# One diffusion block and two attention layers on one core: the opening's loads and waits in a new order, and the attention steps' order on VectorE and GpSimd changed

## What is computed

```python
def _ada(cvec, w_ada, b_ada):
    mod = jax.nn.silu(cvec) @ w_ada + b_ada
    return jnp.split(mod, N_MOD, axis=-1)

def _modulate(x, g, shift, scale):
    return _rmsnorm(x, g) * (1 + scale) + shift

def differential_attention(...):           # 4 heads of the second network, per block of 128 queries
    sc = jnp.einsum('bhcqd,bhckd->bhcqk', qi, k).astype(jnp.float32) * scale
    p = jax.nn.softmax(sc, axis=-1)
    a = p[:, :, 0] - lam * p[:, :, 1]      # two softmaxes, the second times lam, subtracted
    return jnp.einsum('bhqk,bhkd->bhqd', a, vf)
```

## Time and profile before

| | |
|---|---|
| median of 3 runs (lowest, highest) | 3914.33 us (3908.04 to 3921.22) |
| the profiled execution: its own time | 3913.21 us |
| the profiled execution: span | 3911.4 us |
| granted TensorE clock, mean of the span | 0.978 |
| PE busy | 93% |
| DVE, ACT, POOL busy | 29%, 20%, 11% |

### The profile page before, as it was taken

How to read it: one execution, slowest core, us unless ns; L and a number is a source line. 1 busy time by engine, 2 the same in 40 slices (tenths; PEclk the granted TensorE clock), 3 DMA queues, 4 the chain that set the end, 5 groups by cost and what they waited for, 6 DMA issues and landing times.

```text
span 3911.4 us, 33012 instructions
## 1 busy us (share of the span) xinstructions
PE 3627.2 (93%) x12600; PEld 1750.7 (45%) x12600; DVE 1151.3 (29%) x2612; ACT 767.0 (20%) x1772; POOL 428.8 (11%) x393
## 2 busy tenths in 40 slices
PE   8999999999999798788888788999999989999999
PEld 3555555444444433233332344555444545454444
DVE  3355656333201303110111034433221144432211
ACT  2135454223201200000000022222110122221100
POOL 0003324011000000000000002101220021012200
PEclk9899999999999899999999999999999999999999
DMA  8413223112224599999999961012222211122220
GB/s 282 154 61 97 87 72 103 49 56 87 65 65 178 212 409 409 409 409 409 409 409 409 409 236 54 27 44 81 85 76 74 76 54 38 38 92 77 74 81 27
DMA packets 302209, 634.08 MB, mean 162 GB/s; under 512 B 32554, under 2 KB 145818, under 8 KB 301798
## 3 DMA queue, kind: packets, MB, share of 16 engines
q1 hardware_dynamic: 241278, 592.28, 40.7%
q10 hardware_dynamic: 60776, 39.70, 3.7%
HBM read 625.50 MB, written 10.24 MB: 163 GB/s over the span
## 4 chain that ended last, share of the span: by engine, by line
PE 55%; DMA 17%; DVE 3%; SPq 1%; issue 1%; POOL 0%; ACT 0%; DVEq 0%
PE psum L308 27%; DMA arena<-in_w_exp_up_dram 7%; DMA arena<-in_w_exp_gate_dram 6%; PE psum L1638 6%; PE psum L2441 5%; PE psum L2898 4%; PE psum L2934 4%; DMA arena<-in_w_exp_down_dram 4%; PE psum L1462 2%; PE psum L2919 1%; PE psum L1490 1%; PE psum L2367 1%; PE psum L1471 1%; SPq L277 1%; PE psum L2833 1%
## 5 line engine op out<-in xcount | busy, mean ns | idle before, releaser
L308 PE MATMUL psum<-arena 128*128 128x512 f32 (+1 forms) x3200 | 1302.9, 565 | 2.6 <-POOL arena L2040 2.4
L308 PEld LDWEIGHTS psum<-arena 128*128 128x128 f32 x3200 | 609.8, 193 | 675.3 <-issue 653.0
L2441 PE MATMUL psum<-arena 128*64 128x512 f32 x3072 | 692.9, 597 | 141.7 <-DMA arena<-in_w_exp_up_dram 77.1
L2441 PEld LDWEIGHTS psum<-arena 128*64 128x64 f32 x3072 | 232.4, 136 | 583.3 <-issue 567.5
L1638 PE MATMUL psum<-arena 128*128 128x512 f32 x768 | 351.0, 612 | 0.0
L810 PE MATMUL psum<-arena 128*128 128x512 f32 (+1 forms) x768 | 255.9, 491 | 1.1 <-DVE arena L550 1.1
L1638 PEld LDWEIGHTS psum<-arena 128*128 128x128 f32 x768 | 147.0, 195 | 193.4 <-issue 192.5
L1570 DVE CUSTOM_DVE_ANT_0 arena<-psum,arena 128x512 f32<-128x512 f32 (+3 forms) x224 | 113.9, 546 | 391.2 <-PE psum L1462 391.0
L2977 POOL TENSOR_SCALAR arena<-arena 128x512 f32<-128x512 f32 x88 | 138.6, 1576 | 697.7 <-ACT arena L2956 697.7
L810 PEld LDWEIGHTS psum<-arena 128*128 128x128 f32 x768 | 144.4, 191 | 107.9 <-issue 96.1
L2983 DVE SCALAR_TENSOR_TENSOR arena<-arena 128x512 f32<-128x512 f32 x88 | 66.2, 752 | 426.5 <-POOL arena L2977 426.5
(11 more groups left out here) (276 smaller groups left out, 2909.4 us busy)
## 6 DMA issues: line engine op xcount, KB each, us to landing
arena<-in_w_exp_gate_dram SPq DMA_DIRECT2D x128, 1024.0 KB, 18.6
arena<-in_w_exp_up_dram SPq DMA_DIRECT2D x128, 1024.0 KB, 18.5
arena<-in_w_exp_down_dram SPq DMA_DIRECT2D x128, 1024.0 KB, 18.5
arena<-in_w_in_dram SPq DMA_DIRECT2D x64, 1024.0 KB, 5.2
arena<-in_w_up_dram SPq DMA_DIRECT2D x88, 512.0 KB, 4.9
arena<-in_w_ada_dram SPq DMA_DIRECT2D x24, 1024.0 KB, 9.1
arena<-in_w_down_dram SPq DMA_DIRECT2D x20, 1024.0 KB, 5.1
arena<-acs_scratch ACTq DMA_DIRECT2D x64, 256.0 KB, 4.6
```

The source lines that it names most:

```text
L308: mm = pe.matmul(shaped(b, l, r), l, r, start=kt == 0, stop=kt == nkt - 1)
L2441: mm = pe.matmul(banks[n][64 * j:64 * j + 64, :], lhs[:, kt, 64 * j:64 * j + 64], w, start=kt == 0, stop=kt == 2 * nkb - 1)
```

## The change

Opening: SP first loads the identity, then the first `w_ada` block (1, 0), the rest of the constants, `x` in two pieces (the second half first), `ctx`, and after them `w_ada` (0, 0). The four small vectors go to ACT's queue. PE waits for the identity alone before its first transpose, and does the product of (0, 0) after the transposes of `x`. DVE takes the columns of (1, 0) ahead of squaring `x`. Attention: in `dve_att_2`, `weights` stands before `scores`; in `pool_att_2`, `second` has lag 0, not 1. Both serve all three attentions, though `second` acts on differential units only.

```diff
--- before.py
+++ after.py
@@ -564,18 +564,21 @@
             for n in range(2):
                 turned(e, "c", jp, 2 * jp + n, PS.of(("HT", "c", jp))[:, 256 * n:256 * n + 256], HT[:, 2 * jp + n, 512:768], n == 1)
 
-        def sp_vec(sp, groups, key):
+        def load_vec(e, groups, key):
             for col, r, ap, n in vec_src:
                 if col in groups:
-                    sp.dma_start(stage[r:r + n, col * 128:(col + 1) * 128], ap).then_inc(*up(S(f"vec_in{groups[0]}"), by=16))
+                    e.dma_start(stage[r:r + n, col * 128:(col + 1) * 128], ap).then_inc(*up(S(f"vec_in{groups[0]}"), by=16))
             mark(key, S(f"vec_in{groups[0]}"))
 
         def sp_start(sp):
-            sp_vec(sp, (0,), ("vec", 0))
-            sp.dma_start(consts, csrc).then_inc(*up(S("consts_in"), ("consts",), by=16))
+            sp.dma_start(ident, csrc[:, 0:128]).then_inc(*up(S("ident_in"), ("ident",), by=16))
             sp_ada(sp, 1, 0)
+            sp.dma_start(consts[:, 128:], csrc[:, 128:]).then_inc(*up(S("consts_in"), ("consts",), by=16))
+            for i in (2, 0):
+                sp.dma_start(xin[:, i:i + 2, :], xT[:, i:i + 2, :]).then_inc(*up(S(f"x_in{i // 2}"), ("x_in", i), ("x_in", i + 1), by=16))
+            sp.dma_start(cin, A["ctx"].rearrange("a (t p) d -> p (a t) d", p=128)).then_inc(*up(S("c_in"), ("c_in",), by=16))
             sp_ada(sp, 0, 0)
-            sp_vec(sp, (1, 2, 3, 4, 5), ("vec", 1))
+            load_vec(sp, (1, 2, 3, 4, 5), ("vec", 1))
             sp_ada(sp, 1, 1)
             sp_ada(sp, 0, 1)
 
@@ -593,9 +596,7 @@
             act.activation(dst, src, ACT.Copy, bias=0.0, scale=ssq_of[nm][0][:, i:i + 1]).then_inc(*up(S("act_xn"), ("xn", nm, i)))
 
         def act_start(act):
-            for i in range(4):
-                act.dma_start(xin[:, i, :], xT[:, i, :]).then_inc(*up(S(f"x_in{i}"), ("x_in", i), by=16))
-            act.dma_start(cin, A["ctx"].rearrange("a (t p) d -> p (a t) d", p=128)).then_inc(*up(S("c_in"), ("c_in",), by=16))
+            load_vec(act, (0,), ("vec", 0))
             act.wait_ge(*at("col", 0))
             act.wait_ge(*at("cv0"))
             act.activation(cv3[:, :, 0], vmain[:, 56:64], ACT.Silu, bias=0.0, scale=1.0).then_inc(*up(S("act_cv")))
@@ -639,17 +640,17 @@
 
         def dve_start(dve):
             dve_vec(dve, 0)
+            dve_ada_copy(dve, 1, 0, r0bufs[0])
+            dve.wait_ge(*at("col", 0))
+            dve_ada_cols(dve, 1, 0, gpm)
             for i in (2, 3):
                 dve.wait_ge(*at("x_in", i))
                 dve_square(dve, "x", i, xin[:, i, :])
             dve_rstd(dve, "x", *ssq_of["x"], 1024.0)
-            dve_scaled(dve, "x", 0, xin[:, 0, :], xn_x[:, 0, :])
-            dve_ada_copy(dve, 1, 0, r0bufs[0])
-            dve_scaled(dve, "x", 2, xin[:, 2, :], xn_x[:, 2, :])
+            for i in (0, 2):
+                dve_scaled(dve, "x", i, xin[:, i, :], xn_x[:, i, :])
             dve.wait_ge(*at("c_in"))
             dve_square(dve, "c", 1, cin[:, 1, :])
-            dve.wait_ge(*at("col", 0))
-            dve_ada_cols(dve, 1, 0, gpm)
             dve_rstd(dve, "c", *ssq_of["c"], 1024.0)
             dve_scaled(dve, "c", 0, cin[:, 0, :], xn_c[:, 0, :])
             dve_ada_copy(dve, 0, 0, r0bufs[1])
@@ -673,14 +674,15 @@
             pe_turn(pe, ("vec", i), PALL, [stage[0:vec_n[i], i * 128:(i + 1) * 128]], "pe_turn")
 
         def pe_start(pe):
-            pe.wait_ge(*at("consts"))
+            pe.wait_ge(*at("ident"))
             pe.wait_ge(*at("vec", 0))
             pe_vec(pe, 0)
             pe.wait_ge(*at("cv"))
             pe_ada_product(pe, 1, 0)
-            pe_ada_product(pe, 0, 0)
+            pe.wait_ge(*at("consts"))
             pe_ada_cols(pe, 1, 0, r0bufs[0])
             pe_turned_x(pe, 0)
+            pe_ada_product(pe, 0, 0)
             pe_ada_cols(pe, 0, 0, r0bufs[1])
             pe_ada_product(pe, 1, 1)
             pe_turned_c(pe, 0)
@@ -1618,7 +1620,7 @@
                 dve.scalar_tensor_tensor(out=oT2[:, p, :], in0=PS.of(("o2", J.id, p)), scalar=J.gain, in1=hy, op0=ALU.mult, op1=ALU.mult).then_inc(
                     *up(S("dve_oT"), ("free", ("o2", J.id, p)), ("oT2", J.id, p)))
 
-            yield from att2_steps(J, (1, sums), (0, scores), (1, weights), (2, turned), (3, outs), (4, heads))
+            yield from att2_steps(J, (1, sums), (1, weights), (0, scores), (2, turned), (3, outs), (4, heads))
 
         def pool_att_2(pool, J):
             def second(i, u):
@@ -1626,7 +1628,7 @@
                     pool.wait_ge(*at("lam2", J.id, i))
                     pool.tensor_scalar(J.score(i, 1), J.score(i, 1), sv2(i, 1)[:, 2:3], None, ALU.mult).then_inc(*up(S("pool_S1"), ("S2", J.id, i)))
 
-            yield from att2_steps(J, (0, lambda i, u: J.pool_tables(pool, i)), (1, second))
+            yield from att2_steps(J, (0, lambda i, u: J.pool_tables(pool, i)), (0, second))
 
 
 
```

## The result

| | before | after |
|---|---|---|
| median of 4 (lowest, highest) | 3913.4 us (3908.04 to 3921.22) | 3886.6 us (3885.54 to 3892.4) |
| ratio, 95% interval | | 0.9933 [0.9913, 0.9953] |
| profiled execution: its own time, span | 3913.21, 3911.4 | 3887.34, 3885.5 |

The change takes 0.67% off, some 27 us; the interval of the ratio is 8 us to either side. From here on a line L1473, L1579, L1593, L1629 or L1640 is the old L1471, L1577, L1591, L1627 or L1638.

What follows compares the result with a forecast made beforehand. PE, busy 93% of the span, was taken to bound the kernel. Gains of 1 (opening), 4 (neighbourhood attention) and 2 x (9.2 + 2.5) (two layers) summed to 28.4, giving 3886 us, range 3868 to 3903.

Steps and rivals of the forecast that it cites:

- the case that I held likeliest: Whole kernel: the summed gains come as counted, 3886 us (3877 to 3894), chance 0.56.
- After a rope filler: Differential units, rope half: PE's wait of 2.4 us falls to 0.6 and slow fillers speed up; 8.5 us gained a layer.
- After a value filler: Differential units, value half: DVE now waits in line for POOL, so intervals between fillers change; 1.7 us lost a layer.
- Step 16's filler: Differential units, late filler: behind a short wait it takes 7.15 us, not 9.71; 2.4 us gained a layer.
- The other units: Causal layers, non-differential units: four waits for weights become shorter waits for the bank's copy; 2.5 us gained a layer (1 to 5).
- The neighbourhood attention: Neighbourhood attention: four waits shorten by 0.9 us each, 3.6, with the clock 4 us gained (2 to 8).
- The opening: Kernel start: the third block's product, at 29.68 before, starts near 28.5; 1 us gained, or up to 2 lost.
- C: Rival, all three attentions: waits for weights turn into nearly equal waits for the bank; 3908 us, chance 0.09.
- D: Rival, differential units: the chain through POOL also outlasts the rope fillers, so the kernel is slower; 3950 us, chance 0.04.
- A: Rival, mainly value half: POOL's chain is longer than counted or every filler behind it slow; 3900 us, chance 0.17.
- B: Rival, whole kernel: the full clock comes back everywhere; 43 us gained, 3871 us, chance 0.14.
- the clock rule: PE's clock is throttled by default and activity releases it; longer waits then cut a layer's differential gain from 9.2 to 6.4.

Runs made afterwards that it cites:

- e2: Kernel before with only the attention's two new orders (DVE's and POOL's), the opening left old; 3884.92 us.
- e3: Kernel after with POOL's `second` back at lag 1, DVE's weights still ahead of scores; 21 us lost against the kernel after.
- e4: Kernel after with DVE's scores ahead of weights again, `second` still at lag 0; its time met the expectation of 3908 us or more.
- e1: Kernel after with both attention orders put back, so the new opening alone; within 0.15% of the kernel before.
- e11: Kernel before with both new attention orders and the position-bias copies issued later, the opening old; 3876.35 us.
- e5: Kernel after with DVE's copy of the transposed weights moved ahead of the scores; 3856.57 us.
- e12: Kernel after with late position-bias copies, second map multiplied on DVE, and DVE's copy of transposed weights first in the step, ahead of sums; runs 3855.6 to 3870.6 us.

## Why the prediction was right, and which terms were not

3886 was said and 3886.6 measured, the case that I held likeliest. That the attention's new order gives it, and that both halves of it are needed, is shown by e2, e3 and e4. That the sum is within 1 us is luck. The two layers gave 17.7 for my 23.4, the neighbourhood attention 8 to 12 for my 4, and the opening nothing for my 1. The waits went where I said; of the clock I had too much in the layers and too little in the neighbourhood attention. And one of my own signs of being wrong came: rope fillers that "still take 8.8", as those of steps 6 and 16 do. Term by term:

- **After a rope filler, 8.5 us.** Measured from the fillers of the two layer-0 time lines: steps 2 to 4 took 11.12 and take 9.58, 1.5 (I said 1.75); steps 4 to 8 took 28.31 and take 23.61, 4.7 (6.8). From filler 4 to 6 it is 10.55, as I had it (10.8); from 6 to 8 it is 13.06. What failed was "less 1.7 of slow filler" at every step: step 6's stayed at 8.77. And the bank that is late next, for which I took 0.6, costs 0.88, 1.17 and 1.46, growing with the width.
- **After a value filler, 1.7 lost.** 38.35 became 40.91, so 2.6. Intervals 10.14, 10.28, 10.81 and 9.68 against my 10.7, 10.4, 9.9 and 9.1. The wait at step 9 was 2.5, not "up to 4.5", and that at step 13 3.25; the third interval was longer than I had it, with a filler of 5.38 behind it.
- **Step 16's filler, 2.4 gained.** It takes 8.84, and 0.9 was gained in layer 0. In layer 1 it was at the full clock before (7.15, behind a wait of 2.02) and took 8.84 after, so 1.7 was lost. I had read layer 0 alone and counted it twice. "Each such wait is followed by a slow filler" was wrong already by my rows: two of the seven are followed by 3.73. Nor are the seven "all alike": they run from 1.22 to 2.62.
- So the differential half gave 1.5 + 4.7 - 2.6 + 0.9 = **4.5, not 9.2**, in layer 0, just under my lower bound of 5. In layer 1, read in the same way, it gave 1.5 + 4.7 - 1.8 - 1.7 = **2.8**. The wait part was sized rightly: idle time there fell by 8.4, of which 5.0 came back as products running alone, and my own terms without the clock were 1.75 + 3.4 - 1.7 = 3.5. What failed is the clock part, 5.8 in my sum: 1.1 came of it in layer 0, and 0.6 was lost in layer 1. The Trainium skill (page "TensorE: Matmul & The Clock Gate", section "What's actually happening") says that the default state is throttled and activity releases it. From that I had 6.4, and the fillers of steps 14 and 16 slow; in the kernel after they are, in both layers (5.38 and 5.42 at step 14, 8.84 and 8.84 at step 16). The trace agrees in part only: in e2, with the same attention, step 16's filler took 7.15 in layer 0, behind the same gap of 0.34.
- **The other units, 2.5.** From step 17 on 182.16 became 176.25: **5.9**, in both layers. The waits at the four steps, 6.7 in sum, became 4.9, as said (1.8 of gain for my 2.1), and two slow fillers of 5.14 and 5.01 became 3.73, 2.7 more. In all, idle time fell by 2.3 and busy time by 3.6, at a clock of 1.00 for 0.98: I counted "a little from the clock" and it was the larger part. With 1.5 lost ahead of step 2, where no unit is turned yet, layer 0 comes to 9.0 for my 11.7.
- **The neighbourhood attention, 4.** Measured 8.4 to 11.8 in the pairs e1 to e2 and before to after, 10.0 in e4 to e3. Its waits for weights and copy fell from 10.1 to 6.2, and that 3.9 is what I had forecast (3.6); the rest is the clock, which in the 200 us from 863 on is 1.00, and was 0.97:

```profile
863.00:1063.00 200.00, 195.76 (x657) 92.94 (x654) 59.04 (x176) 58.87 (x114) 18.52 (x32) 1.00 0.23 78
```

- **The opening, 1.** The profile after seems to say just that, 44.06 for 45.11, but for another reason. "Both paths give about 28.5" was wrong: the normalised `x`, which I had at 20.3, lets the transposes begin at 21.89, these take 3.65, the block (0, 0) starts at 25.46 for my 22, and the third block at 30.27. It is the loss that I had as a condition ("if the normalised `x` slips"): 0.7 us, where e11 has the third block at the full clock too.

Of the rivals, C named the right next wait, the bank, and the wrong price for it: at 0.88 to 1.46 it does not take the gain after a rope filler. But the copy was also waited for 17.1 us by the transposes, mostly in the steps without a filler, and e5 shows that all of it together, with the clock, is worth 28. I had treated these waits as what stays. D did not come: PE's rope fillers outlast the chain. A's mechanism, slow fillers behind every wait, came in part, and B's, the clock everywhere, came outside the differential units. By the clock rule my sum would have been 3891.6 and not A's 3900; that is within my own case, so the total cannot tell the two.

## What to carry to other kernels

In an engine's fixed order, look at what each instruction waits for. Let none that waits for another engine's filler stand ahead of one whose input is long there: the change, e5 and e12 are the same rule, obeyed twice and broken once. A removed wait is worth its own length and what the clock gives back behind it, and the second can be nothing (in the differential units here) or more than the first (in the neighbourhood attention). Count it for each repetition of a layer from that one's own rows, since the same wait was followed by a slow filler in one and a fast one in the other. A list of waits counts idle time only: a product that runs alone where two could run together is a wait that it does not show, so compare starts. A start that comes 1 us earlier in one profile proves nothing when a piece ahead of it ran at another clock: compare at the same clock, or time the edit alone.

## What the hardware showed that I had not expected

- 16 products of 128x512 take 7.15 us at the full clock, and took 8.77 behind a gap of 0.26 us among small products, with no long wait near (step 6, after). In the ten layers of the five kernels with that gap it was 8.8 eight times, and in the eight layers of the four kernels without it 7.15 each time.
- The products of two score tiles, of 32 rows each, start together in the kernel before and in every kernel with the copy ahead of the scores, and up to 1.46 us apart in every kernel with the weights ahead of the scores and the copy behind them. The profile lists at most 0.34 of that as a wait.
- A multiplication of 128x512 by a column in fp32 took GpSimd 1.57 us and VectorE 0.49; with the hand-overs 1.85 against 0.72 from the start of the product with lambda to the start of the weights.
- The eight copies of the bias table, 465 KB each, filled the DMA engines' time at 194 GB/s (with what ran beside them) and took 15.1 us from issue to landing, by the median. With them there TensorE waited 1.3 to 3.1 us for a weight transfer in nine profiles, and not at all in the five with them later.
- Stages whose instructions are the same differ by up to 3 us between two kernels' profiles (layer 0 is 474.9 before and 471.7 in e1), so a term under that size is not told from one profile.
